# Routing stage of a two-block transformer kernel: whole-u logits, both halves of u turned to tokens, the few experts' columns gathered half by half

## The chip, the cores and the metric

One Trainium2 chip, one core. The time is the device time of one execution in microseconds (us). The core's engines run their own instruction streams and meet at semaphores: TensorE (PE, with its weight loads PEld), VectorE (DVE), ScalarE (ACT), GpSimd (POOL, not used here) and SyncE (SP), which issues the weight transfers.

## The reference, cut to what matters

The model has two blocks of two layers each, on 256 tokens of width 1024, in float32. The last feed-forward of the second block is a mixture of 8 experts with 2 chosen for each token:

```
h = rms_norm_2(x, norm_ffn_g) * (1.0 + sc2) + sh2
logits = h @ router_w                       # 256 x 8
top_v, top_i = lax.top_k(logits, 2)
probs = jax.nn.softmax(top_v, axis=-1)
gates = sum(one_hot(top_i, 8) * probs[..., None], axis=-2)
for e in range(8):
    out = out + gates[..., e:e+1] * ((silu(h @ w1[e]) * (h @ w3[e])) @ w2[e])
x = x + g2 * out
```

Everything before it (three mixing branches, convolutional feed-forwards, linear attention, one dense feed-forward) is not touched.

## The kernel before

Activations lie transposed: `u` is 8 tiles `k` of 128 channels x 256 tokens. A large product is made of three matmuls in the type fp32r: every operand is cut into a high half (rounded to fp32r) and a low half (what is left), and high x high, high x low and low x high are added (`mm3`). For the weights, SP loads units of 128 x 1024 (512 KB) into a ring of 6 buffers, ACT rounds each unit to `w_high` (`high_to`, L1672), DVE subtracts to get `w_low` (`low_to`, L2176), and PE uses the pair. The split units have 6 buffers of their own. A ring buffer is free when the low half is made, a split buffer when PE has multiplied the unit. All orders are written out by hand: every engine's program is a fixed list, and the named steps in `STEPS` are counted by semaphores.

The routing stage stands between the last normalization and the experts:

- The normalization (`rms`, DVE L2217; ACT L1716 and L1719). For each `k` DVE makes `normed`, ACT makes `u_high`, then the whole `u` in float32 (written over `sq`, the first 2048 columns of the arena), and DVE makes `u_low`.
- `route` on PE. The logits are `u_high` and `u_low` times the router in full float32, 32 matmuls of 8 columns (8 tiles `k`, two halves of the tokens, two parts). Then `by_token0` and `by_token1` turn the whole `u` to token rows (8 transposes each, L1502). Between them stand five small matmuls (`counts`), which count how many tokens each expert has.
- DVE meanwhile takes the two best experts of each token (`second`, `chosen`). After `counts` it sorts the experts by their number of tokens (`order`), and makes `pick`, a 0/1 matrix tokens x slots for four groups of 128 slots, and `spread_tok`, its transpose with the gates.
- SP waits for `order` before it loads the first unit of an expert (L3103), since the order says which expert's weights come first.
- `few0` to `few7` gather: `u_tok` (float32) times `pick` (float32) gives 128 x 512 columns in one bank for each `k`. ACT rounds each to `few_high` (L2055), DVE subtracts to get `few_low` (L2208).
- The experts. The three with the most tokens run on all 256 tokens (18 passes of 6 units, `q` = 0 to 17), the other five on gathered slots (30 passes). `up(q)` multiplies 4 units, `turn` transposes the hidden tile, `down` multiplies 2 units.
- After `up(0)` stands `route_back`: 10 transposes of `spread_tok` (L1527), which ACT takes out as `spread_slot` (L2062). They are needed from the first gathered expert on.
- ACT's and DVE's programs for the experts begin with pass 1: first the Silu of pass 0 (L2074) and `hidden`, then the four units of `up(1)`.

Functions are shown below with the line numbers of the profile before.

## Time and profile before

| | us |
|---|---|
| median of 3 timed runs | 2533.5 (2531.13 to 2535.11) |
| the profiled execution's own time | 2517.57 |
| its span | 2516.1 |
| PE busy | 2304.6 (92% of the span) |
| DVE busy | 1596.2 (63%) |
| ACT busy | 1178.8 (47%) |
| DMA, mean | 170 GB/s |
| normalization and routing, from the last squares to the first full-rate pass | 1896 to 1963 |

The page has PE at the head of the chain that ended last (77% of the span), then DVE (14%) and ACT (4%). A float32 matmul (4 passes over the array) is recorded as two instructions, so 64 records are 32 matmuls; fp32r matmuls have one record each. A matmul's duration covers its way through the array and overlaps with the next one's; what one costs in a stream is the distance from start to start. "PEclk" is the granted clock of PE: 0.50 is 1.2 GHz, 1.00 is 2.4 GHz.

### The profile page before, as it was taken

What the parts mean: (1) busy time and instruction counts of PE and PEld (TensorE: products, weight loads), DVE (VectorE), ACT (ScalarE), POOL (GpSimd) and SP (SyncE); (2) the same over time, 40 slices, a digit from 0 to 9 for tenths busy, and PEclk for the clock granted to TensorE, in tenths of its full rate; (3) what the DMA queues carried; (4) which work ended last, traced back from release to release, by engine and by line L of the source; (5) the groups of instructions that cost most, each with busy time, mean ns of one, the idle gap of its engine ahead of it and who ended that gap; (6) DMA issues with size and microseconds to landing.
All of it is one profiled execution on the core that took longest, in us unless ns stands there. A gap on an engine that the chain in (4) does not pass through costs nothing.

```text
span 2516.1 us, 45037 instructions
## 1 busy us (share of the span) xinstructions
PE 2304.6 (92%) x19087; PEld 2076.5 (83%) x19087; DVE 1596.2 (63%) x2425; ACT 1178.8 (47%) x1717; POOL 0.2 (0%) x4
## 2 busy tenths in 40 slices
PE   7889788899988887988998989999989999999998
PEld 7669788899976777888998979998977788887776
DVE  5537776677763687576775656555654444568886
ACT  5234534455552355355554435445333434456665
POOL 0000000000000000000000000000000000000000
PEclk9999898999999999899998989999987999999999
DMA  5674333355446533253553414554312555569895
GB/s 201 224 257 157 113 106 105 130 183 191 139 173 261 197 118 116 86 175 121 193 192 100 134 59 168 185 190 137 118 34 84 184 176 183 190 237 324 321 330 197
DMA packets 118634, 427.06 MB, mean 170 GB/s; under 512 B 13344, under 2 KB 16160, under 8 KB 118304
## 3 DMA queue, kind: packets, MB, share of 16 engines
q1 hardware_dynamic: 116544, 422.34, 48.9%
q8 instruction: 150, 2.46, 0.4%
q10 hardware_dynamic: 1888, 1.84, 0.2%
q14 instruction: 52, 0.43, 0.0%
HBM read 423.08 MB, written 1.05 MB: 169 GB/s over the span
## 4 chain that ended last, share of the span: by engine, by line
PE 77%; DVE 14%; ACT 4%; issue 2%; DMA 2%; ACTq 0%; SPq 0%; DVEq 0%
PE bank L764 76%; DVE w_low L2176 4%; DVE arena L2208 4%; DMA ring<-in_weights 1%; DVE arena L2217 1%; DVE y_mix L2208 1%; ACT w_high L1672 1%; DVE arena L2678 1%; PE bank L1562 1%; ACT arena L1935 1%; DVE small L2676 0%; DVE arena L2214 0%; DVE arena L2212 0%; DVE arena L2227 0%; ACT arena L1880 0%
## 5 line engine op out<-in xcount | busy, mean ns | idle before, releaser
L2176 DVE TENSOR_TENSOR w_low<-ring,w_high 128x1024 fp32r<-128x1024 f32 x700 | 820.1, 1220 | 146.8 <-ACT w_high L1672 146.7
L764 PE MATMUL bank<-u_high,w_high 128*128 128x256 f32 x2576 | 743.0, 288 | 30.0 <-DVE u_low L2208 23.3
L1672 ACT ACTIVATE w_high<-ring 128x1024 fp32r<-128x1024 f32 x700 | 696.0, 1050 | 134.3 <-PE bank L764 128.0
L764 PE MATMUL bank<-u_low,w_high 128*128 128x256 f32 x2576 | 735.1, 285 | 0.0
L764 PE MATMUL bank<-u_high,w_low 128*128 128x256 f32 x2576 | 734.3, 285 | 0.0
L764 PEld LDWEIGHTS bank<-u_high,w_high 128*128 128x128 f32 x2576 | 499.7, 194 | 42.5 <-issue 39.5
L764 PEld LDWEIGHTS bank<-u_low,w_high 128*128 128x128 f32 x2576 | 499.7, 194 | 0.1
L764 PEld LDWEIGHTS bank<-u_high,w_low 128*128 128x128 f32 x2576 | 498.9, 194 | 0.0
L764 PE MATMUL bank<-arena 64*64 64x64 f32 (+8 forms) x4488 | 258.3, 253 | 78.8 <-DVE arena L2217 22.8
L764 PEld LDWEIGHTS bank<-arena 64*64 64x64 f32 (+3 forms) x4488 | 218.9, 154 | 124.7 <-issue 66.5
L764 PE MATMUL bank<-w_high,u_high 128*128 128x256 f32 (+1 forms) x480 | 166.5, 347 | 5.1 <-DVE w_low L2176 5.1
L2208 DVE TENSOR_TENSOR arena<-arena 128x256 f32<-128x256 f32 (+4 forms) x215 | 139.4, 665 | 46.3 <-ACT arena L1981 21.3
L764 PE MATMUL bank<-hid_high,w_high 128*128 128x256 f32 x528 | 150.0, 284 | 15.3 <-DVE hid_low L2208 15.3
L764 PE MATMUL bank<-w_high,u_low 128*128 128x256 f32 (+1 forms) x480 | 163.1, 340 | 0.0
L764 PE MATMUL bank<-w_low,u_high 128*128 128x256 f32 (+1 forms) x480 | 162.8, 339 | 0.0
L764 PE MATMUL bank<-hid_low,w_high 128*128 128x256 f32 x528 | 149.5, 283 | 0.0
L764 PE MATMUL bank<-hid_high,w_low 128*128 128x256 f32 x528 | 149.3, 283 | 0.0
L2208 DVE TENSOR_TENSOR turned_low<-bank,turned_high 128x256 fp32r<-128x256 f32 (+1 forms) x66 | 24.9, 399 | 161.4 <-ACT turned_high L2084 161.4
L2084 ACT ACTIVATE turned_high<-bank 128x256 fp32r<-128x256 f32 (+1 forms) x66 | 22.2, 365 | 223.6 <-PE bank L1562 223.6
L2217 DVE SCALAR_TENSOR_TENSOR arena<-bank,params,arena 128x255 f32<-128x255 f32 (+1 forms) x204 | 85.6, 476 | 50.5 <-ACT arena L1979 32.1
L1678 ACT ACTIVATE arena<-bank 128x512 f32<-128x512 f32 (+1 forms) x72 | 42.1, 584 | 159.8 <-PE bank L764 159.7
L764 PEld LDWEIGHTS bank<-hid_high,w_high 128*128 128x128 f32 x528 | 101.7, 193 | 16.4 <-issue 16.4
(281 smaller groups left out, 3091.1 us busy)
## 6 DMA issues: line engine op xcount, KB each, us to landing
ring<-in_weights SPq DMA_DIRECT2D x534, 512.0 KB, 4.5
ring<-in_moe SPq DMA_DIRECT2D x264, 512.0 KB, 5.3
const<-in_const SPq DMA_DIRECT2D x1, 2619.0 KB, 16.2
x_res<-in_x SPq DMA_DIRECT2D x2, 512.0 KB, 4.8
out<-x_res ACTq DMA_DIRECT2D x2, 512.0 KB, 3.0
const<-in_par ACTq DMA_DIRECT2D x1, 462.0 KB, 3.4
params<-in_par ACTq DMA_DIRECT2D x1, 247.0 KB, 7.9
small<-in_pos SPq DMA_DIRECT2D x1, 128.0 KB, 16.0
```

The lines of the kernel that those rows point to most:

```text
L764: return pe.matmul(out, lhsT, rhs, start=start, stop=stop, skip_group_check=loose)
L1562: ins = pe.transpose(bank(q, tile)[:, f * P:(f + 1) * P], hid_e[q % 2][tile][:, f * P:(f + 1) * P], c_("ident"))
L1672: act.activation(WH[:, ORDER.slot[cut], :], weights("s", cut), Copy).then_inc(s_hi, 1)
L1678: act.activation(job.dst, held(job), Copy).then_inc(s_out["act"], 1)
L1935: act.activation(L_c[a][:, h, :], L_c[a][:, h, :], Exp, bias=neg_max[a][:, h:h + 1], accum_out=exp_sum[a][:, h:h + 1]).then_inc(*c.mark(f" ...
L2084: act.activation(HTH[q % 2][tile][:, 0:n], psum[4 + 2 * (q % 2) + tile][:, 0:n], Copy)\
L2176: dve.tensor_tensor(WL[:, b, :], weights("s", cut), WH[:, b, :].bitcast(f32), SUB).then_inc(s_lo, 1)
L2208: dve.tensor_tensor(out, a, b, op).then_inc(*t.mark(name))
L2217: dve.scalar_tensor_tensor(out, a, s, b, op0, op1).then_inc(*t.mark(name))
L2678: dve.match_replace(work_[:, a, 0:n], top8, work_[:, a, 0:n], -3e30).then_inc(*d.mark())
```

## The change

- The whole `u` is made first for all `k` (`u0` to `u7`), then `u_high` for all `k`; on DVE all eight `normed` come first, then all `u_low`.
- The logits are whole `u` times the router: 16 float32 matmuls.
- `u_high` and `u_low` are both turned to token rows (32 transposes, four groups of 8, in banks 4 to 7) and written as fp32r to `U_TOK` by ACT, 8 copies of 128 x 512. The counts stand between the second group and the third.
- The gather is made of 32 fp32r matmuls: 16 results (`few0` to `few15`), of which 0 to 7 are the high halves and 8 to 15 the low halves. They go through 8 banks, so the last eight wait until an earlier result has been taken out (`X_BANK`).
- The even results are copied by ACT, the odd ones by DVE. The four units of `up(0)` are split between them, and two units of `up(1)` at the end.
- ACT runs a Silu on one column after the Exp, and `spread_slot` is taken out after the Silu of pass 0.
- `silu_e` lies elsewhere in the arena, and `pick` is of type fp32r.

```diff
@@ STEPS @@
-        "logits by_token0 counts by_token1 few0 ... few7 spread0 spread1 spread2",
+        "logits by_token0 by_token1 counts by_token2 by_token3 few0 ... few15 spread0 spread1 spread2",
@@ build @@
+    U_TOK = [pairs2(over_arena(f"by_token_{n}", 8 * T * h, 2048)) for h, n in enumerate(("high", "low"))]
+    X_FEW = [(XH, XL)[n // 8][:, n % 8, :] for n in range(16)]
+    X_BANK = (0, 1, 2, 3, 4, 5, 6, 7, 4, 5, 6, 7, 0, 1, 2, 3)
+    TOK_BANK = ((4, 5), (6, 7), (4, 5), (6, 7))
@@ PE route @@
-                pe.wait_ge(*R.dve(f"low{k}"))
+                pe.wait_ge(*E.act(f"u{k}"))
                 for a in TWO:
-                    for part in (UH, UL):
-                        ins = mm(psum[1][:, a * 8:a * 8 + 8], part[:, k, a * P:(a + 1) * P].bitcast(f32), rw[:, k, :], ...)
+                    ins = mm(psum[1][:, a * 8:a * 8 + 8], sq[:, k, a * P:(a + 1) * P], rw[:, k, :], ...)
...
+            pe.wait_ge(*R.dve(f"low{KT - 1}"))
+            by_token(0, 0)
+            by_token(0, 1)
             pe.wait_ge(*E.dve("chosen"))
...
-            by_token(1)
+            pe.wait_ge(*E.act("tok3"))
+            by_token(1, 0)
+            by_token(1, 1)
             pe.wait_ge(*E.dve("pick"))
-            pe.wait_ge(*E.act("by_token"))
-            for k in range(KT):
+            pe.wait_ge(*E.act("tok7"))
+            for n in range(16):
+                if n > 7:
+                    old = X_BANK.index(X_BANK[n])
+                    pe.wait_ge(*(E.act, E.dve)[old % 2](f"x{old}"))
                 for a in TWO:
-                    ins = mm(psum[k][:, :], u_tok[:, a, k * P:(k + 1) * P], pick[:, a, :], a == 0, a == 1)
+                    ins = mm(psum[X_BANK[n]][:, :], U_TOK[n // 8][:, a, (n % 8) * P:(n % 8 + 1) * P], pick[:, a, :], ...)
@@ PE experts, up @@
-                        pe.wait_ge(*E.dve(f"low{5 + 2 * q}"))
+                        pe.wait_ge(*E.act(f"x{8 + 2 * q}"))
+                        pe.wait_ge(*E.dve(f"x{9 + 2 * q}"))
@@ ACT route @@
+            by_token(0)
+            by_token(1)
             act.wait_ge(*E.dve("second"))
             act.activation(r_p1, r_p1, Exp).then_inc(*E.act.mark("second"))
+            act.activation(unused, eps, Silu).then_inc(*E.act.mark())
+            for n in range(2, 8):
+                by_token(n)
+            for n in range(0, 16, 2):
+                act.wait_ge(*E.pe(f"few{n}"))
+                act.activation(X_FEW[n], psum[X_BANK[n]][:, :], Copy).then_inc(*E.act.mark(f"x{n}"))
+                if n in (2, 6, 10, 12):
+                    high_to(ORDER.up[0][(2, 6, 10, 12).index(n)])
+            high_to(ORDER.up[1][1])
@@ ACT experts @@
                 silu(q - 1)
+                if q == 1:
+                    route_back(of_route)
@@ DVE route @@
-            for k in range(KT):
-                dve.wait_ge(*E.act(f"high{k}"))
-                tt(d, XL[:, k, :], psum[k][:, :], XH[:, k, :].bitcast(f32), SUB, f"low{k}")
-                if k in (3, 5, 7):
-                    low_to(ORDER.up[0][k // 2 - 1])
-            low_to(ORDER.up[0][3])
+            for n in range(1, 16, 2):
+                dve.wait_ge(*E.pe(f"few{n}"))
+                copy(d, X_FEW[n], psum[X_BANK[n]][:, :], f"x{n}")
+                if n in (3, 7, 11, 13):
+                    low_to(ORDER.up[0][(3, 7, 11, 13).index(n)])
+            low_to(ORDER.up[1][1])
```

On PE, from the logits to the first unit of `up(0)`, the kernel before has this (the pair of router rows stands 16 times in all; `arena` is `u_tok`, `const` the identity):

```order
L764 MATMUL bank<-router,u_high 128x8
L764 MATMUL bank<-router,u_low 128x8
L1502 MATMUL bank<-const,arena 128x128 x8
L764 MATMUL bank<-small,steady 128x8 x2
L764 MATMUL bank<-small,const 128x8
L764 MATMUL bank<-small,steady 128x8
L764 MATMUL bank<-small,const 128x8
L1502 MATMUL bank<-const,arena 128x128 x8
L764 MATMUL bank<-arena 128x512 x16
L764 MATMUL bank<-w_high,u_high 128x512
```

The changed kernel has this:

```order
L777 MATMUL bank<-steady,arena 128x1 x10
L777 MATMUL bank<-const,rstd 128x128 x2
L777 MATMUL bank<-router,arena 128x8 x16
L1515 MATMUL bank<-const,u_high 128x128 x16
L777 MATMUL bank<-small,steady 128x8 x2
L777 MATMUL bank<-small,const 128x8
L777 MATMUL bank<-small,steady 128x8
L777 MATMUL bank<-small,const 128x8
L1515 MATMUL bank<-const,u_low 128x128 x16
L777 MATMUL bank<-few_pick,by_token_high 128x512 x16
L777 MATMUL bank<-few_pick,by_token_low 128x512 x16
L777 MATMUL bank<-w_high,u_high 128x512
```

The router rows have become one run of 16. The transposes stand in two groups of 16, the first of `u_high`, the second of `u_low`, and the first 16 gather matmuls read the high halves.

On ACT, from the last `u_high` to the second unit of `up(0)`, the kernel before has this (L2051 takes the token rows out, L2055 the gathered columns):

```order
L1716 ACTIVATE u_high<-arena,mod 128x256
L1719 ACTIVATE arena<-arena,mod 128x256
L2048 ACT_TABLE_LOAD
L2048 ACTIVATE small<-small 128x2
L2051 ACTIVATE arena<-bank 128x512 x4
L2055 ACTIVATE few_high<-bank 128x512 x4
L1672 ACTIVATE w_high<-ring 128x1024
L2055 ACTIVATE few_high<-bank 128x512 x2
L1672 ACTIVATE w_high<-ring 128x1024
L2055 ACTIVATE few_high<-bank 128x512 x2
L1672 ACTIVATE w_high<-ring 128x1024 x2
```

The changed kernel has this, from the whole `u` on (L1734 makes it, L2071 takes out token rows, L2083 gathered columns, L1693 splits units):

```order
L1734 ACTIVATE arena<-arena,mod 128x256 x8
L1740 ACTIVATE u_high<-arena,mod 128x256 x8
L2071 ACTIVATE by_token_high<-bank 128x512 x2
L2077 ACT_TABLE_LOAD
L2077 ACTIVATE small<-small 128x2
L2078 ACT_TABLE_LOAD
L2078 ACTIVATE steady<-steady 128x1
L2071 ACTIVATE by_token_high<-bank 128x512 x2
L2071 ACTIVATE by_token_low<-bank 128x512 x4
L2083 ACTIVATE few_high<-bank 128x512 x2
L1693 ACTIVATE w_high<-ring 128x1024
L2083 ACTIVATE few_high<-bank 128x512 x2
```

Two copies of token rows now stand ahead of the Exp (L2077) and its table load, and a second table load (L2078, for the Silu) stands between them and the other six.

Further down on ACT, around the end of `up(0)`, the kernel before has this (L2062 is `spread_slot`, L2074 the Silu of pass 0, L2084 the turned hidden tile):

```order
L1672 ACTIVATE w_high<-ring 128x1024 x2
L2062 ACTIVATE arena<-bank 128x512 x2
L2062 ACTIVATE arena<-bank 128x256
L2074 ACT_TABLE_LOAD
L2074 ACTIVATE arena<-bank 128x256 x2
L1672 ACTIVATE w_high<-ring 128x1024 x4
L2084 ACTIVATE turned_high_61<-bank 128x256
L2084 ACTIVATE turned_high_62<-bank 128x256
```

The changed kernel has this (L2104 is the Silu, L2092 `spread_slot`, L2114 the turned tile):

```order
L1693 ACTIVATE w_high<-ring 128x1024
L2083 ACTIVATE few_low<-bank 128x512
L1693 ACTIVATE w_high<-ring 128x1024 x2
L2104 ACTIVATE arena<-bank 128x256 x2
L2092 ACTIVATE arena<-bank 128x512 x2
L2092 ACTIVATE arena<-bank 128x256
L1693 ACTIVATE w_high<-ring 128x1024 x2
L2114 ACTIVATE turned_high_64<-bank 128x256
L2114 ACTIVATE turned_high_65<-bank 128x256
```

The first two units of `up(1)` have moved ahead of the Silu and of `spread_slot`, and the table load is gone from here.

## Rows read from the trace of the kernel before

**Rows 1.** Page: PE's busy us, share, instructions; unit splits' busy, mean ns, idle.
```profile
PE 2304.6 (92%) x19087; PEld 2076.5 (83%) x19087; DVE 1596.2 (63%) x2425; ACT 1178.8 (47%) x1717; POOL 0.2 (0%) x4
...
L2176 DVE TENSOR_TENSOR w_low<-ring,w_high 128x1024 fp32r<-128x1024 f32 x700 | 820.1, 1220 | 146.8 <-ACT w_high L1672 146.7
...
L1672 ACT ACTIVATE w_high<-ring 128x1024 fp32r<-128x1024 f32 x700 | 696.0, 1050 | 134.3 <-PE bank L764 128.0
```

**Rows 2.** Busy time of each engine by stretch, then granted clock, DMA share, GB/s.
```profile
1896.00:1950.00 54.00, 47.75 (x183) 36.02 (x183) 27.05 (x84) 19.16 (x36) 0.00 (x0) 0.75 0.28 98
...
1956.00:2260.00 304.00, 303.85 (x1399) 247.33 (x1398) 159.50 (x190) 130.39 (x189) 0.00 (x0) 0.99 0.56 195
```

**Rows 3.** Chain of waits, 1880 to 2000 us: start, duration, work.
```profile
1899.08 13.82 PE bank L764 x64
...
1955.49 7.76 PE bank L764 x24
...
1963.69 16.80 PE bank L764 x72
```

**Rows 4.** Timeline of PE, 1896 to 1960 us: start, duration, work, [idle before].
```profile
1912.76 1.95 PE L1502 MATMUL bank<-const,arena 128*128 128x128 f32 x8
1914.62 1.02 PE L764 MATMUL bank<-small,steady 128*128 128x8 f32 x4
...
1922.69 15.43 PE L764 MATMUL bank<-arena 128*128 128x512 f32 x32 [3.96 <-DVE arena L2217]
...
1949.18 1.25 PE L1527 MATMUL bank<-const,arena 128*128 128x128 f32 x10
1955.49 0.77 PE L764 MATMUL bank<-w_high,u_high 128*128 128x512 f32 x1 [5.06 <-DVE w_low L2176]
1956.06 0.63 PE L764 MATMUL bank<-w_low,u_high 128*128 128x512 f32 x1
...
1959.04 0.63 PE L764 MATMUL bank<-w_high,u_low 128*128 128x512 f32 x1
```

**Rows 5.** Timeline of ACT, 1896 to 1960 us.
```profile
1898.00 0.51 ACT L1716 ACTIVATE u_high<-arena,mod 128x256 fp32r<-128x256 f32 x1 [1.61 <-DVE arena L2217]
...
1904.51 1.28 ACT L2048 ACT_TABLE_LOAD   x1
...
1914.74 1.08 ACT L2051 ACTIVATE arena<-bank 128x512 f32<-128x512 f32 x2 [0.65 <-PE bank L1502]
...
1926.14 0.60 ACT L2055 ACTIVATE few_high<-bank 128x512 fp32r<-128x512 f32 x1 [6.29 <-PE bank L764]
...
1949.81 1.36 ACT L2062 ACTIVATE arena<-bank 128x512 f32<-128x512 f32 x3 [9.16 <-PE bank L1527]
1951.19 1.28 ACT L2074 ACT_TABLE_LOAD   x1
1952.49 0.66 ACT L2074 ACTIVATE arena<-bank 128x256 f32<-128x256 f32 x2
```

**Rows 6.** Timeline of DVE, 1896 to 1960 us.
```profile
1916.96 0.17 DVE L2217 SCALAR_TENSOR_TENSOR small<-bank,const 128x8 f32<-128x8 f32 x1 [1.41 <-PE bank L764]
...
1922.55 2.65 DVE L2214 TENSOR_SCALAR arena<-const,small 128x128 f32<-128x128 f32 x10
1926.77 0.69 DVE L2208 TENSOR_TENSOR few_low<-bank,few_high 128x512 fp32r<-128x512 f32 x1 [1.56 <-ACT few_high L2055]
```

**Rows 7.** Timeline of SP's DMA queue, 1917 to 1926 us.
```profile
1918.65 3.00 SPq L3109 DMA_DIRECT2D ring<-in_moe  x6
```

**Rows 8.** Busy time by stretch, around the steps of PE's granted clock.
```profile
1898.00:1899.00 1.00, 0.00 (x0) 0.00 (x0) 0.82 (x3) 1.00 (x3) 0.00 (x0) 0.65 0.00 0
...
1925.00:1926.00 1.00, 1.00 (x3) 0.35 (x2) 0.20 (x1) 0.00 (x0) 0.00 (x0) 0.70 0.94 356
1928.00:1930.00 2.00, 2.00 (x6) 0.95 (x5) 0.69 (x1) 0.88 (x2) 0.00 (x0) 1.00 0.22 88
1959.00:1960.00 1.00, 1.00 (x4) 0.82 (x3) 0.00 (x0) 0.00 (x0) 0.00 (x0) 0.63 0.72 270
```

More of the change, by code:

```diff
@@ L368 @@
         "normed7 low6 low7",
+    "ffn3_pe":
+        "sum spread",
+    "ffn3_act":
+        "-1 sq0 sq1 sq2 sq3 sq4 sq5 sq6 sq7 root high0 high1 high2 high3 high4 high5 high6 high7",
+    "ffn3_dve":
+        "inverse normed0 normed1 normed2 normed3 normed4 normed5 normed6 normed7 low0 low1 low2 low3 low4 "
+        "low5 low6 low7",
     "add2_pe":
@@ L411 @@
     "route_pe":
-        "logits by_token0 counts by_token1 few0 few1 few2 few3 few4 few5 few6 few7 spread0 spread1 spread2",
+        "logits by_token0 by_token1 counts by_token2 by_token3 few0 few1 few2 few3 few4 few5 few6 few7 few8 "
+        "few9 few10 few11 few12 few13 few14 few15 spread0 spread1 spread2",
     "route_act":
-        "-7 u second -3 by_token high0 high1 high2 high3 high4 high5 high6 high7 spread0 spread1 spread2",
+        "u0 u1 u2 u3 u4 u5 u6 u7 tok0 tok1 second -1 tok2 tok3 tok4 tok5 tok6 tok7 x0 x2 x4 x6 x8 x10 x12 x14 "
+        "spread0 spread1 spread2",
     "route_dve":
-        "-5 second -3 chosen -8 order -22 pick -9 spread low0 low1 low2 low3 low4 low5 low6 low7",
+        "-5 second -3 chosen -8 order -22 pick -9 spread x1 x3 x5 x7 x9 x11 x13 x15",
     "tables_act":
@@ L688, in build @@
     space(8 * T)
-    u_tok = pairs2(new(2048))
-    back = u_tok
+    back = pairs2(new(2048))
     XH, XL = (over_arena(n, 16 * T + 4096 * h, 4096).rearrange("p (k s) -> p k s", k=KT)
@@ L709, in build @@
     of_conv = [[stage("conv", layer * FF_GROUPS + j) for j in range(FF_GROUPS)] for layer in range(LAYERS)]
-    of_mix2, of_lin, of_ffn2 = (
-        [stage(name, layer) for layer in range(LAYERS)] for name in ("mix2", "lin", "ffn2"))
+    of_mix2, of_lin = (
+        [stage(name, layer) for layer in range(LAYERS)] for name in ("mix2", "lin"))
+    of_ffn2 = [stage("ffn2", 0), stage("ffn3", 0)]
     of_add2 = stage("add2", 0)
@@ L1574, in down @@
                     pe.wait_ge(*E.act("spread2"))
-                    pe.wait_ge(*E.dve("low3"))
                 for tile in tiles(q):
@@ L1710, in rms @@
         def rms(R, add_of=None, whole=None):
+            for k in range(KT) if whole is not None else ():
+                act.wait_ge(*R.dve(f"normed{k}"))
+                act.activation(sq[:, k, :], un[:, k, :], Ident, bias=add_of(k)).then_inc(*whole.act.mark(f"u{k}"))
             for k in range(KT):
@@ L2265, in rms @@
                 stt(d, out[:, k, :], X[:, k, :], g_of(k), mean_of(R), MUL, MUL, f"normed{k}")
-                if k and out is un:
+                if k and out is un and R is not of_ffn2[-1]:
                     low(R, k - 1, un, add_of)
-            if out is un:
-                low(R, KT - 1, un, add_of)
+            for k in range(KT) if R is of_ffn2[-1] else (KT - 1,) if out is un else ():
+                low(R, k, un, add_of)
         def branch_a(A, M, side, layer):
```

51 lines of the change are left out of this document (23 added, 28 removed).

## Prediction, made before the changed kernel was run

> **What bounds the kernel now.** I read the page first, then busy time by stretch. PE is busy for 92% of the span, so it bounds the kernel as a whole [rows 1]. Around the change this is different: from 1896 to 1950 us PE is "busy" for 47.75 of 54 us, but at a mean granted clock of 0.75, with DMA at a share of 0.28, while the expert passes behind it keep PE busy for 303.85 of 304 us at 0.99 [rows 2]. So the routing stage is a serial piece in which PE either waits or runs slowly. What it saves passes to the end: the passes that follow hang on PE alone, and each is 16.80 us for 72 matmuls, 0.233 us each [rows 3].
>
> The chain of waits and the timelines then give the stage's order: `u` ready, logits 1899.08 to 1912.76, transposes and counts, DVE's sorting until `pick`, gather from 1922.69, `up(0)`, `route_back` at 1949.18, and 5.06 us of waiting for `w_low` before `up(1)` starts at 1955.49 [rows 3, 4, 6]. `up(0)` is 48 matmuls, so it began 48 x 0.233 = 11.2 us before 1949.18, at 1938.0.
>
> **Logits.** 32 matmuls took 1912.76 - 1899.08 = 13.7 us, 0.427 each, at 1.2 GHz: the clock fell during 1898 to 1899, when PE had nothing to do [rows 4, 8]. Sixteen are left, 6.8 us. They start when the first whole `u` is there. Before, the first logits waited for `normed`, high (0.51) and low on DVE; now for one ACTIVATE after `normed`, which ends at 1898.5 [rows 5]. ACT makes 16 of these in 6.5 us, 0.40 each [rows 5]; two matmuls for each `k` take 0.85, so PE sets the pace. Logits end at 1898.55 + 6.83 = 1905.4, 7.4 us earlier. The reordered halves don't hold them: high0 comes after u7, at 1901.2, and low7 ends at 1905.0, just ahead of the wait in front of the first transposes. If that wait came out 0.5 us late, this would cost 0.5.
>
> **Transposes and counts.** Eight transposes take 1.86 us (1912.76 to 1914.62) [rows 4]. Sixteen now stand ahead of the counts: 1905.4 + 3.72 = 1909.1. From the first count to DVE's next step were 2.34 us (1914.62 to 1916.96) [rows 4, 6], so DVE goes on at 1911.45, 5.5 us earlier than before. Is it free by then? ACT takes out two token copies first (they began 1.98 us after the first transpose and took 1.08 [rows 4, 5]: until 1908.5), then the Exp's table load, 1.28 [rows 5], which earlier lay in idle time at 1904.51; the Exp ends at 1910.0. DVE's six small steps for the gates come behind it; all 18 small steps between logits and counts took 2.8 us before (1912.76 until 1.41 before 1916.96 [rows 4, 6]), so 1.1 us is my estimate for the six: 1911.1. The margin is 0.35 us. From there to `pick` are 5.7 us as before (1916.96 to the gather's release at 1922.69) [rows 4, 6]: ready at 1917.15. SP's first six expert loads move with it, from 1918.65 to 1913.1 [rows 7].
>
> **The second half of the tokens.** After the Exp comes the Silu's table load with its one-column Silu (0.2, an estimate below the 0.33 of a 256-column one in row 1952.49), 1.5 us: until 1911.5. The next two copies end at 1912.6. PE waits for them (`tok3`), turns `u_low` from 1912.6 to 1916.3, and ACT's last copy (`tok7`) ends at 1917.5. That is 0.4 us after `pick`, so the token copies now release the gather, at 1917.5 instead of 1922.69: 5.2 us gained here. The chain from the logits to this point goes through ACT, and what ACT takes longer than I say comes on top one for one.
>
> The table loads are where a page speaks against this change. The trace has a load at 1951.19 directly behind an ACTIVATE row that ends at 1951.17, and the Silu behind the load at 1952.49: 1.28 in all with no gap on either side [rows 5]. The Trainium skill ("ScalarE: Activation LUTs", section "What ACT_TABLE_LOAD costs") puts a switch of sets at 1283 ns for the load and about 1380 ns for a drain. By that rule the loads' duration agrees and the drain doesn't show. With the drain twice on the new path the gather would start 2.8 us later. I go by the row.
>
> **The gather.** In float32, 16 matmuls took from 1922.69 to 1938.0, 15.3 us; the first result went to ACT at 1926.14, after two matmuls of 1.7 us [rows 4, 5]. Now there are 32 fp32r matmuls of 512 columns, a form that `up` shows at both clocks: 0.426 from start to start between 1956.06 and 1959.04 (seven of them), 0.233 at full clock [rows 3, 4]. Bounds for this term are 32 x 0.233 = 7.5 us (full clock from the start) and 32 x 0.427 = 13.7 us (low throughout). In between: after PE took up dense work at 1922.69, the clock rose at about 1925.6 (0.70 in that microsecond), and after 1955.49 at about 1959.7 (0.63 in that one) [rows 8], so 2.9 and 4.3 us. The gather's first matmuls have the form of the second case, so I take 4.3 us: 10 matmuls at 0.427 and 22 at 0.233, 9.4 us, until 1926.9.
>
> Can ACT and DVE follow? A copy on ACT is 0.60 and on DVE about 0.69 (that of `few_low` from a bank; the copy has the same 128 x 512) [rows 5, 6]. DVE has the ten `spread_tok` steps first, 2.65 [rows 6], until 1919.7; few1 is then just done. Walking both programs with units of 1.05 (ACT) and 1.22 (DVE) [rows 1]: x5 is out at 1923.7, when `few9` wants its bank after `few8` at 1923.7; x7 at 1924.3 before `few11`; x9, for which `up(0)` waits, at 1925.9. So `few15` ends at 1927.0 with next to nothing lost. Low halves of `up(0)`'s units come at 1923.1, 1925.4, 1927.6 and 1929.3, and PE wants them at 1927.0, 1929.8, 1932.6 and 1935.4. The loads: before, DMA fell to a share of 0.22 in 1928 to 1930, so six units had landed some 10 us after 1918.65 [rows 7, 8]; now that is by 1923.5, and the fourth unit is first touched at 1926.7. `up(0)` starts at 1927.0 instead of 1938.0: 11.0 us gained so far.
>
> **`route_back` and `up(1)`.** Before, ACT took `spread_slot` out, loaded the Silu's table, ran the Silu, and only then split the first unit of `up(1)`; PE waited 5.06 us [rows 4, 5]. Now both first units are split by 1932, ahead of the end of `up(0)` at 1938.2. That wait goes. What is late next? PE goes from `route_back` (10 transposes, 1.25) at 1939.4 straight into 24 matmuls; the second two units need their high halves, which ACT makes after the Silu (0.66) and `spread_slot` (1.36, from 1939.6): they are split by 1944.6 on DVE, and PE wants them at 1945.5. So nothing. The wait also let the clock fall: the 24 matmuls took 7.76 us [rows 3] against 24 x 0.233 = 5.6. Those 2.2 us go too, if the clock stays up.
>
> **Sum.** End of the first half of `up(1)`: 1963.25 before, 1927.0 + 11.2 + 1.25 + 5.6 = 1945.05 now. By terms: 5.2 (gather starts) + 5.8 (gather shorter) + 5.06 (wait) + 2.2 (clock) = 18.2 us. Against the profiled execution, 2517.57, this gives 2499.4. The median of the timed runs lies 15.9 us above the profiled time; I carry the difference over: 2533.5 - 18.2 = 2515.3.
>
> **Rivals.**
>
> A, a table switch costs more than its load, as in the page above, or ACT is late otherwise: the gather starts at 1920.3, saving 15.4, 2518.1. The row speaks against it. 8%.
>
> B, the clock stays at 1.2 GHz for the whole gather. For it: the last eight results wait for banks, and transposes and copies ahead leave PE gaps. Price 13.7 - 9.4 = 4.3, and half of `up(0)` at the low clock another 24 x 0.193 = 4.6. Saving 9.3 to 13.9: 2519.6 to 2524.2. Against: the float32 gather and `up(1)` both brought the clock back within 4.3 us [rows 8], and the walk above finds no bank wait over 0.1 us. The Trainium skill ("TensorE: Matmul & The Clock Gate", section "A second HAM failure mode: psum-queue depth-cycling") tells of a kernel whose cycling through PSUM banks left short idle times and a clock that went up and down; the gather now cycles through banks in this way, and no row of before has such cycling with fp32r matmuls. 13%.
>
> C, slower: the clock stays low through the gather, `up(0)`, `route_back` and `up(1)`. Gather 13.7, `up(0)` 20.5, ten transposes 2.3, 24 matmuls 10.2: from 1917.5 to 1964.2, 1 us behind the 1963.25 of before, and each further pass of 72 adds 13.9. It decides if the clock is not up by about 1964; with one more pass 2533.5 + 1.0 + 13.9 = 2548.4. `up(0)` has no bank to wait for, and dense passes always raised the clock [rows 2, 8]. 2%.
>
> D, more is saved: the clock rises right at the gather's start, or doesn't fall for the logits. Then the gather's end is held by x9 at 1925.9 and the transposes lose up to 3.5 us, of which ACT's copies leave about 1. Saving 19 to 20.5: 2513 to 2514.5. 7%.
>
> E, the stage is shorter but the saving is given back behind it: the gathered experts load more than the dense ones, and a memory bound there would not move. But loads are tied to the ring's buffers, so they move with PE, and nothing has a fixed time. A saving under 5 us: 2528.5 to 2533.5. 4%.
>
> The forecast, a saving of 16.5 to 19, has 66%.
>
> **How the numbers follow.** Likeliest 2515. The range holds A, D, most of B, and some 2 us in which a median may differ: 2510 to 2523. About 0.2% (5 us) is what a measurement of this kernel can tell from no change: faster takes the forecast, A, B and D, 94%, less 1 for what I haven't seen, 93%; same is E, 4%; slower is C and the unseen, 3%.
>
> **What would show it.** In the changed profile: 32 router records (16 matmuls) over 6.8 us; gather starting 17 to 20 us after the logits' start (19.0 by my sum); few results from start to end in 9 to 10 us; no wait above 1 us between `up(0)` and `up(1)`; first half of `up(1)` in 5.6 us. It would be wrong if the gather's matmuls stood 0.427 apart to the end, if a gap stood around the table loads, or if `up(0)` waited for a copy on DVE.

## The result and the profile after

| | before | after |
|---|---|---|
| median with the prediction's comparison | 2534.06 us (4 runs) | 2509.28 us (2508.04 to 2515.12, 4 runs) |
| ratio, 95% interval | | 0.9905 [0.9888, 0.9923] |
| repeated | | 0.9914 [0.9892, 0.9936] and 0.9931 [0.9910, 0.9952] |
| all executions in this study, mean and standard error | 2531.6, 0.5 (75 executions, 2522.6 to 2543.9) | 2510.3, 1.1 (16, 2504.2 to 2519.0) |
| profiled execution's span | 2516.1 | 2506.6 |
| the routing stage in it | 66.51 | 48.54 |

The change makes the kernel faster, as forecast, but the median fell just below the range (2510 to 2523). "Stage" is here the time from the start of the spread of the last normalization's roots to the end of the first half of `up(1)` in the chain of waits: 1896.74 to 1963.25 us before [rows 3] and 1904.09 to 1952.63 after. The "spread" is the step in which PE copies each token's root to all rows, just ahead of the whole `u`. It is this row of the chain before:

```profile
1896.74 0.72 PE bank L764 x4
```

PE's timeline of the changed kernel (start, duration, work, idle before), with the rows that answer to [rows 4]:

```profile
1904.09 0.71 PE L777 MATMUL bank<-const,rstd 128*128 128x128 f32 x4 [0.65 <-DVE rstd L2255]
1905.92 7.00 PE L777 MATMUL bank<-router,arena 128*128 128x8 f32 x32 [1.11 <-ACT arena L1734]
1912.76 3.36 PE L1515 MATMUL bank<-const,u_high 128*128 128x128 f32 x16
...
1919.89 3.67 PE L1515 MATMUL bank<-const,u_low 128*128 128x128 f32 x16 [2.75 <-ACT by_token_high L2071]
1924.83 6.00 PE L777 MATMUL bank<-few_pick,by_token_high 128*128 128x512 f32 x16 [1.27 <-DVE arena L2246]
1930.67 4.07 PE L777 MATMUL bank<-few_pick,by_token_low 128*128 128x512 f32 x16
...
1945.78 1.25 PE L1548 MATMUL bank<-const,arena 128*128 128x128 f32 x10
...
1952.47 0.60 PE L1584 MATMUL bank<-const,arena 128*128 128x128 f32 x4
```

The 16 logits matmuls (32 records) take 1912.76 - 1905.92 = 6.84 us against 13.7. From the logits' start to the gather's are 18.91 us against 23.61. The gather runs from 1924.83 to 1934.58 (48 x 0.233 ahead of 1945.78), 9.75 us against 15.3. `route_back` goes into `up(1)` with no wait.

The chain of waits (start, duration, work) shows the end of it, with 24 matmuls in 5.60 us where [rows 3] had 7.76:

```profile
1924.83 21.11 PE bank L777 x80
...
1947.03 5.60 PE bank L777 x24
```

ACT's timeline, for [rows 5], and DVE's, for [rows 6]:

```profile
1914.75 1.09 ACT L2071 ACTIVATE by_token_high<-bank 128x512 fp32r<-128x512 f32 x2 [2.90 <-PE bank L1515]
1915.85 1.28 ACT L2077 ACT_TABLE_LOAD   x1
1917.15 0.20 ACT L2077 ACTIVATE small<-small 128x2 f32<-128x2 f32 x1
1917.37 1.28 ACT L2078 ACT_TABLE_LOAD   x1
1918.66 0.20 ACT L2078 ACTIVATE steady<-steady 128x1 f32<-128x1 f32 x1
1918.77 1.07 ACT L2071 ACTIVATE by_token_high<-bank 128x512 fp32r<-128x512 f32 x2
...
1923.60 1.09 ACT L2071 ACTIVATE by_token_low<-bank 128x512 fp32r<-128x512 f32 x2 [0.62 <-PE bank L1515]
```

```profile
1909.09 3.27 DVE L2249 SCALAR_TENSOR_TENSOR u_low<-arena,mod,u_high 128x256 fp32r<-128x256 f32 x8 [1.02 <-ACT u_high L1740]
...
1917.38 0.17 DVE L2244 TENSOR_SCALAR small<-small 128x2 f32<-128x2 f32 x1 [2.80 <-ACT small L2077]
...
1918.37 0.16 DVE L2249 SCALAR_TENSOR_TENSOR small<-bank,const 128x8 f32<-128x8 f32 x1
...
1923.42 0.61 DVE L2249 SCALAR_TENSOR_TENSOR few_pick<-const,small,few_pick 128x128 fp32r<-128x128 f32 x2
1923.96 2.65 DVE L2246 TENSOR_SCALAR arena<-const,small 128x128 f32<-128x128 f32 x10
```

Two table loads of 1.28 us stand on ACT with nothing on either side of them but the ACTIVATEs. DVE waited 2.80 us for the Exp and used the counts, which were there, as soon as the gates were done. The last token copies ended at 1924.69, after `pick` at 1924.03, and the gather began at 1924.83. (Its row names DVE's L2246 as the releaser, which makes `spread_tok` and which the gather doesn't wait for; the same row of after_again, below, names the token copies.)

Busy time by stretch, with the granted clock in the third place from the end, around the clock's steps, for [rows 8]:

```profile
1905.00:1906.00 1.00, 0.08 (x1) 0.09 (x1) 1.00 (x3) 0.65 (x2) 0.00 (x0) 0.72 0.00 0
1915.00:1916.00 1.00, 1.00 (x9) 1.00 (x7) 0.00 (x0) 0.98 (x3) 0.00 (x0) 0.66 0.00 0
1919.00:1920.00 1.00, 0.11 (x1) 0.11 (x2) 0.86 (x7) 0.84 (x2) 0.00 (x0) 0.55 0.00 0
1929.00:1930.00 1.00, 1.00 (x6) 0.77 (x5) 0.97 (x2) 0.84 (x2) 0.00 (x0) 0.83 0.60 242
```

The clock falls at about 1905.4, in the idle time between the spread and the logits, rises in the first group of transposes at about 1915.7, falls again at about 1919.1, 2.0 us into the 2.75 us in which PE stood idle, and rises at about 1929.3, 4.5 us into the gather. Before, it stayed low from 1898.3, ahead of the logits, until 1925.6.

### The profile page after: what moved, and what is told of

The parts are those of the page before. It is cut to its first block, busy times and chain, and to the rows that moved or that the text cites. A ratio compares the mean times of both kernels' runs of the same rounds, so it can differ in the third digit from the quotient of the medians.

```text
span 2506.6 us, 45010 instructions
## 1 busy us (share of the span) xinstructions
PE 2296.7 (92%) x19071; PEld 2075.5 (83%) x19071; DVE 1595.7 (64%) x2425; ACT 1181.1 (47%) x1722; POOL 0.2 (0%) x4
## 4 chain that ended last, share of the span: by engine, by line
PE 78%; DVE 14%; ACT 4%; issue 3%; DMA 2%; ACTq 0%; SPq 0%; DVEq 0%
PE bank L777 76%; DVE w_low L2208 4%; DVE arena L2240 4%; DMA ring<-in_weights 1%; DVE arena L2249 1%; DVE y_mix L2240 1%; ACT w_high L1693 1%; DVE arena L2710 1%; PE bank L1584 1%; ACT arena L1956 1%; DVE arena L2246 0%; DVE small L2708 0%; DVE arena L2259 0%; DVE arena L2244 0%; ACT arena L1901 0%
## 5 line engine op out<-in xcount | busy, mean ns | idle before, releaser
L1693 ACT ACTIVATE w_high<-ring 128x1024 fp32r<-128x1024 f32 x700 | 696.5, 1050 | 132.0 <-PE bank L777 125.3
L777 PE MATMUL bank<-arena 64*64 64x64 f32 (+5 forms) x4456 | 245.1, 251 | 79.9 <-issue 23.1
L777 PEld LDWEIGHTS bank<-arena 64*64 64x64 f32 (+2 forms) x4456 | 214.5, 155 | 117.4 <-issue 63.3
L2240 DVE TENSOR_TENSOR arena<-arena 128x256 f32<-128x256 f32 (+4 forms) x215 | 139.4, 665 | 46.3 <-ACT arena L2002 21.3
L777 PE MATMUL bank<-hid_high,w_high 128*128 128x256 f32 x528 | 150.1, 284 | 15.3 <-DVE hid_low L2240 15.3
L2114 ACT ACTIVATE turned_high<-bank 128x256 fp32r<-128x256 f32 (+1 forms) x66 | 22.2, 365 | 218.9 <-PE bank L1584 218.9
## 6 DMA issues: line engine op xcount, KB each, us to landing
small<-in_pos SPq DMA_DIRECT2D x1, 128.0 KB, 15.9
```

The lines of the kernel that those rows point to most:

```text
L777: return pe.matmul(out, lhsT, rhs, start=start, stop=stop, skip_group_check=loose)
L1693: act.activation(WH[:, ORDER.slot[cut], :], weights("s", cut), Copy).then_inc(s_hi, 1)
L2114: act.activation(HTH[q % 2][tile][:, 0:n], psum[4 + 2 * (q % 2) + tile][:, 0:n], Copy)\
L2240: dve.tensor_tensor(out, a, b, op).then_inc(*t.mark(name))
```

## Experiments

Stages are measured as above, times of runs are means with standard errors. The one comparison of all is with before: stage 66.5, mean 2531.6.

**The two kernels again.** No edit.

> The kernel before, unchanged, run as if it were a new one. The profile of before was 2517.57 us, its timed runs 2531 to 2535, and I carried that difference over to the changed kernel. Theory 1: the profiled execution was one draw from a spread that comes from the PE clock in the first 1900 us (each low stretch costs about half its length); the routing stage itself is the same in every execution. Then the profile here shows the stage (from the spread of the last normalization's roots to the end of the first half of up(1)) at 66.5 us, plus or minus 2, and a whole time of 2520 to 2535, with the missing part before the stage. Theory 2: the stage itself is longer in typical runs of before (72 to 75 us, the clock rising later), so that the change is worth 24 us there. Rival: before has no spread, and an execution of it is at 2517 whenever it is profiled and at 2531 when it is not; then all profiles are some 15 us under the timed runs.

> The kernel before again, for one more profile. Two profiles of it have the stage at 66.5 us and the unchanged work ahead of it at 1896.7 and 1912.6 us. If the part ahead is what varies: stage 66.5 again, start of the stage anywhere from 1895 to 1917. If before's own stage is longer in typical executions (that would explain why timed means of changed kernels lie some 4 us further below before than their stages do): 68 us or more, by a longer low stretch in the gather, as in tail_alone's profile (30.7 us low, gather 16.9).

> As before_p3: one more profile of the kernel before. Stage 66.5 by the one view, 68 us or more by the other.

> The changed kernel again, beside before. Theory 1: the stage is 48.5 us (measured in the first profile), plus or minus 2, and what differs between executions lies ahead of it; timed ratio 0.990 to 0.993. Theory 2: ratio 0.990 with a stage of 48.5 and one of before of over 70.

> The changed kernel once more, for its stage and its mean. If what the timed runs show beyond the stage (21.9 against 18.0 to 19.6 us so far) is the scatter of the unchanged part: stage 46.9 to 48.6 us, mean of the runs 2510 to 2514, so that the difference to before comes down towards 18 to 20. If it is a lasting gain outside the stage: mean 2509 to 2510 again and a difference of 21 to 23.

| profile of | stage starts at | stage | rest behind it | span | mean clock of the execution |
|---|---|---|---|---|---|
| before, first | 1896.74 | 66.51 | 552.9 | 2516.1 | 0.951 |
| before_again | 1912.55 | 66.48 | 552.9 | 2531.9 | 0.944 |
| before_p3 | 1905.85 | 66.55 | 553.5 | 2525.9 | 0.946 |
| before_p4 | 1909.78 | 66.69 | 552.5 | 2529.0 | 0.945 |
| after, first | 1904.09 | 48.54 | 554.0 | 2506.6 | 0.951 |
| after_again | 1908.79 | 46.95 | 552.8 | 2508.5 | 0.947 |
| after_p3 | 1904.63 | 46.93 | 552.7 | 2504.3 | 0.951 |

The chain of waits in before_again, at its start and end of the stage:

```profile
1912.55 0.72 PE bank L764 x4
...
1971.27 7.76 PE bank L764 x24
```

The stage of before is the same within 0.2 us in four profiles, so theory 2 of the first expectation fell, and so did the rival: before_again's own profiled execution took 2533.39. What varies is the unchanged work ahead of the stage, by 16 us, and the mean clock of PE varies with it: 0.951 over 2516 us is 2 x 0.049 x 2516 = 247 us at the low clock, 0.944 over 2532 is 284. Half of the 37 us between them is 18, against 15.8 measured. The profile on which I built the forecast was faster than all 75 executions of before in this study.

The changed kernel's stage comes in two lengths, 48.5 and 46.9 us, and the gather makes 1.3 of the 1.6 between them: it takes 9.75 us in the first profile, 8.44 in the other two. PE's timeline in after_again:

```profile
1929.23 3.91 PE L777 MATMUL bank<-few_pick,by_token_high 128*128 128x512 f32 x16 [1.26 <-ACT by_token_low L2071]
1932.98 0.73 PE L777 MATMUL bank<-few_pick,by_token_low 128*128 128x512 f32 x2
1934.36 3.48 PE L777 MATMUL bank<-few_pick,by_token_low 128*128 128x512 f32 x14 [0.64 <-DVE few_high L2252]
```

There the clock fell at about 1924.1 and was up again at about 1927.5, before the gather began (a mean of 0.74 from 1927 to 1928, 1.00 from 1928 on), so the second low stretch took 3.4 us and not 10.2. At the full clock the gather still took 8.44 us and not 7.5, since PE waited 0.64 us for a bank that DVE was late to empty: DVE's ten `spread_tok` steps lasted until 1931.3. after_p3 has the same rows, with the same 0.64.

**One part alone, on the kernel before.** In logits_alone only the logits come from the whole `u`:

```diff
-                pe.wait_ge(*R.dve(f"low{k}"))
-                    for part in (UH, UL): (two matmuls)
+                pe.wait_ge(*E.act("u" if k == KT - 1 else f"u{k}"))
+                    (one matmul on sq[:, k, ...])
```

> The kernel before with one part of the change alone: the logits from whole u (16 matmuls that wait for u of their k), all else as before. If the term is 16 matmuls of 0.427 us and nothing else: logits 6.8 us instead of 13.7, stage 66.5 - 6.8 = 59.6 us (less 0.1 or so for the earlier start), all later pieces unchanged, time 7 us less than before. Rival: the low clock stretch, 27.3 us long in both profiles of before, ends or moves with the shorter piece, so that the transposes and the gather come out at the full clock and the part is worth 10 us or more.

Its PE timeline:

```profile
1908.62 6.99 PE L764 MATMUL bank<-router,arena 128*128 128x8 f32 x32 [1.51 <-ACT arena L1718]
...
1925.40 15.50 PE L764 MATMUL bank<-arena 128*128 128x512 f32 x32 [3.96 <-DVE arena L2216]
```

Stage 59.67, 6.8 us less, as the sum said; the gather still takes its 15.3 us, with the low clock at its start. Mean 2521.1 (1.2), 10.5 below before, 3.7 (1.3) more than the stage gives.

In tail_alone only the tail is changed (early Silu, `spread_slot` behind the first Silu, two units of `up(1)` ahead, and `silu_e` elsewhere in the arena):

```diff
+            act.activation(unused, eps, Silu)          # behind the Exp
-            high_to(ORDER.up[0][3])
+            high_to(ORDER.up[1][1])                    # DVE: low_to, the same
+                if q == 1: route_back(of_route)        # behind silu(0)
```

> The kernel before with only the tail changed: early Silu on one column, spread_slot behind the Silu of pass 0, two units of up(1) split ahead. By the forecast 5.06 us of waiting and 2.2 us of low clock go: stage 59.2 us, time 7.3 less than before. undo_tail gave 7.4 to 9.0 us of stage in the changed kernel. Rival: the Silu's load, 1.28 us, now stands between the Exp and the token copies and delays the gather, 6.0 us net.

```profile
1937.46 17.07 PE L764 MATMUL bank<-arena 128*128 128x512 f32 x32 [3.96 <-DVE arena L2222]
```

The gather still starts 23.60 us after the logits, so the Silu's load costs nothing there. But its 32 records take 17.07 us against 15.43 [rows 4]: the clock rose 6.2 us into it in this execution, against 2.9 before. Stage 60.94; without that 1.65 us it would be 59.3 by this reckoning, the 7.2 us of the sum; this is worked out, not measured. Mean 2521.7 (1.2).

**One part undone, on the changed kernel.** undo_tail takes the same lines back:

> Changed kernel with the tail as before: no early Silu, spread_slot taken out ahead of the Silu, the units of up(1) split only behind it. By my sum 5.1 us of waiting and 2.2 us of low clock come back: stage 55.7 us, time 7.2 us more than the changed kernel. Rival: with the gather shorter, ACT has idle time and the wait is covered: under 2 us.

```profile
1948.63 1.25 PE L1548 MATMUL bank<-const,arena 128*128 128x128 f32 x10
...
1954.94 0.77 PE L777 MATMUL bank<-w_high,u_high 128*128 128x512 f32 x1 [5.06 <-DVE w_low L2203]
...
1963.04 0.60 PE L1584 MATMUL bank<-const,arena 128*128 128x128 f32 x4
```

Stage 55.75 against the 55.7 expected: the wait of 5.06 us for `w_low` is back to the hundredth, and the 24 matmuls behind it take 8.1 us. The clock was low for the first 5.5 us of its gather, so the profile of the changed kernel to set beside it is the first, and the part is worth 7.2. Mean 2518.5 (1.0), 8.2 above the changed kernel.

undo_logits computes the logits from the halves again, in the changed order:

```diff
-                pe.wait_ge(*E.act(f"u{k}"))
+                pe.wait_ge(*R.dve(f"low{k}"))
+                    for part in (UH, UL): (two matmuls)
```

> The changed kernel with the logits from the two halves (32 matmuls, waiting for each low half). By the sum: logits 13.7 us instead of 6.8, and they start at the first low half, 2.8 us later than at the first whole u, since the changed order has all highs behind all u: stage 9 to 10 us longer (56 to 58), time 9 to 10 us more. Rival: only 6.8 us, as in logits_alone the other way round.

```profile
1912.92 0.71 PE L777 MATMUL bank<-const,rstd 128*128 128x128 f32 x4 [0.65 <-DVE rstd L2256]
1918.46 0.59 PE L777 MATMUL bank<-router,u_high 128*128 128x8 f32 x2 [4.82 <-DVE u_low L2250]
...
1932.13 3.32 PE L1516 MATMUL bank<-const,u_high 128*128 128x128 f32 x16
```

Stage 59.05, 10.5 to 12.1 more than the changed kernel's (10.5 against the first profile, whose gather had the clock low as long as here), a little over the 9 to 10: the logits take 13.67 and start 5.54 us after the spread instead of 1.83, 3.7 later where I had 2.8. Mean 2521.3 (1.6), 11.0 more. With logits that need the halves, the new order (all highs behind all `u`) costs 3.2 us against before, where they started 2.34 us after the spread.

**The gather.** gather_f32 keeps everything but the type:

```diff
-    pick = pairs2(over_arena("few_pick", pick_at, 2 * 4 * P))
+    pick = pairs2(at(pick_at, 2 * 4 * P))
-    U_TOK = [pairs2(over_arena(f"by_token_{n}", 8 * T * h, 2048)) ...]
+    U_TOK = [pairs2(at(8 * T * h, 2048)) for h in TWO]
```

> The changed kernel with the turned halves and pick in float32, so that the 32 gather matmuls run in float32 (0.86 us each at the full clock, by before's gather) instead of fp32r. By the sum the type is what pays for gathering twice: gather 28 to 31 us instead of 8.4 to 9.8, stage 67 to 70, time about 2529 to 2532, no better than before. Rival: copies and banks set the gather's pace, and it grows by less than 15 us.

```profile
1924.68 27.71 PE L777 MATMUL bank<-arena 128*128 128x512 f32 x64 [1.26 <-ACT arena L2071]
```

The row has the 64 records of the 32 matmuls. From 1924.68 to `up(0)` are 27.5 us, 0.86 a matmul, and the stage is 65.99. Mean 2529.7 (1.1): nearly all that the change brings is gone. In fp32r a gather matmul of 512 columns takes 0.233 us where one in float32 takes 0.86, so twice the matmuls still take 8.4 to 9.75 us against 15.3.

No run gathers the old way with the rest of the change in place, so what doubling the gather is worth with all that comes with it (16 more transposes, four more token copies, the new order) is shown by no run. An estimate from the stages, if the parts add: before less logits_alone's 6.8 and the tail's 7.2 is 52.4, and the changed kernel has 46.9 to 48.5, so 4 to 5.5 us. From the other side it is nothing: 48.5 plus 10.5 (undo_logits) plus 7.2 (undo_tail) is 66.3, against 66.5 of before. The gather in halves seems to pay only together with the logits from the whole `u`.

one_engine has ACT copy all 16 results:

```diff
-            for n in range(0, 16, 2):
+            for n in range(16):        # ACT; DVE's copies go
```

> The changed kernel with all 16 gathered results copied by ACT; DVE only splits. ACT then has 16 x 0.50 + 4 x 1.05 = 12.2 us from the first result on, before the last result; x8 and x9 come out about 8 us after the first result. By my walk banks for few8 to few15 come later and up(0) waits for x9: gather to up(0) 11 to 12 us instead of 8.4 to 9.8, and the units of up(0), split in between, come just in time; stage 1.5 to 3 us longer. Rival (the clock sets the gather's length): the same stage within 0.5 us.

```profile
1928.21 3.88 PE L777 MATMUL bank<-few_pick,by_token_high 128*128 128x512 f32 x16 [1.27 <-DVE arena L2246]
1932.49 1.72 PE L777 MATMUL bank<-few_pick,by_token_low 128*128 128x512 f32 x6 [0.40 <-ACT few_high L2083]
1934.89 2.60 PE L777 MATMUL bank<-few_pick,by_token_low 128*128 128x512 f32 x10 [0.69 <-ACT few_high L2083]
```

PE waited 0.40 and 0.69 us for banks; gather 9.12 us, stage 47.69, mean 2509.5 (0.9, 4 runs). The clock was up before this gather began, as in after_again and after_p3, so those are the ones to compare with: 0.7 us more than their 8.44, where I had expected 1.5 to 3. The second engine matters little: with it PE still waits 0.64 us for a bank, without it 1.09.

**What holds the changed stage.** exp_first moves the Exp:

```diff
-            by_token(0)
-            by_token(1)
             act.wait_ge(*E.dve("second"))
             act.activation(r_p1, r_p1, Exp)
+            for n in range(4):
+                by_token(n)
             act.activation(unused, eps, Silu)
-            for n in range(2, 8):
+            for n in range(4, 8):
```

> Changed kernel with ACT's Exp ahead of the token copies (its table load in the idle time ahead of the logits' end) and the Silu's load behind the fourth copy. In the changed kernel's profile DVE waited 2.80 us for the Exp, and PE 2.75 us for the fourth copy. If these waits are the path: pick 1.3 us earlier, u_low's transposes 2.6 earlier, gather starts 2.0 us earlier, stage 46.5 us, time 2 us less. Rival (the counts on PE would hold DVE anyway, since they come behind 16 transposes): under 0.5 us.

```profile
1916.57 1.97 PE L1515 MATMUL bank<-const,u_low 128*128 128x128 f32 x16 [0.16 <-ACT by_token_high L2071]
1922.17 5.42 PE L777 MATMUL bank<-few_pick,by_token_high 128*128 128x512 f32 x16 [3.64 <-DVE few_pick L2249]
...
1928.60 3.48 PE L777 MATMUL bank<-few_pick,by_token_low 128*128 128x512 f32 x14 [0.54 <-DVE few_high L2252]
```

The waits went (2.75 us for the copy became 0.16) and the gather began 17.21 us after the logits instead of 18.91 or 18.6, 1.4 to 1.7 of the 2.0 expected. PE now waited 3.64 us for `pick`. The clock fell at about 1922.0, at the end of that idle time, and rose at about 1925.4:

```profile
1919.00:1921.00 2.00, 0.00 (x0) 0.00 (x0) 1.86 (x12) 0.97 (x2) 0.00 (x0) 1.00 0.92 307
1921.00:1923.00 2.00, 0.83 (x2) 0.73 (x3) 1.97 (x9) 0.00 (x0) 0.00 (x0) 0.75 0.97 324
...
1925.00:1927.00 2.00, 2.00 (x10) 1.61 (x9) 1.26 (x3) 1.86 (x3) 0.00 (x0) 0.89 0.99 391
```

The gather took 9.75 us, with the clock low for its first 3.3 and the wait of 0.54 for a bank, so the stage, 46.86, is no better than the better profiles of the changed kernel; mean 2510.7 (1.7).

evict_first is exp_first with two changes more: it also puts `spread_tok` behind DVE's copies, and each unit of `up(0)` one pair of results later.

> exp_first with DVE's ten spread_tok steps (2.65 us) behind the copies of gathered columns, and each unit of up(0) split one pair of results later, since few9 waited 0.54 us for x5 in exp_first. If banks hold the gather: gather 9.2 us instead of 9.75 at the same clock, stage 46.2. If the clock alone sets the gather's length: 9.7 to 9.8, or 8.4 to 8.5 when the low stretch is 3.4 us; no change in the stage.

Gather 8.81 us, below the 9.2 of the first view and between the two cases of the second; stage 45.70. No wait for a bank is left in it, and the clock was low for its first 3.0 us, nearly as long as in exp_first, so most of the 0.9 us between the two is what waiting for banks cost there. Mean 2511.1 (1.1).

evict_first_warm is evict_first with one more change: it fills the idle time in front of the gather (evict_warm_2 is the same kernel again):

```diff
+        def busy(n):
+            for _ in range(n):
+                mm(psum[3][:, 0:256], UH[:, 0, 0:P], UH[:, 0, :], True, True)
             by_token(1, 1)
+            busy(24)
             pe.wait_ge(*E.dve("pick"))
```

> evict_first with 24 fp32r matmuls of 256 columns, whose result nobody reads, on PE between the last transposes and the gather, where PE was idle for 3.6 us in exp_first (24 x 0.117 = 2.8 us at the full clock, 5.1 at the low one). If the idle time is what lets the clock fall in front of the gather: no low stretch behind the first one, gather 7.6 to 8.6 us, stage 44.5 to 45.5, time 1 to 2 us less than evict_first. Rival: the clock is low there already, the fill runs 5.1 us and pushes the gather back: stage 1 to 2 us longer.

> evict_first_warm again beside the changed kernel on one chip. Its stage was 44.3 us against 48.5 and 46.9 of the changed kernel; the timed runs of the first call did not show it (2509.2). If the stage's gain passes to the end: stage 44.0 to 44.6, and 2.5 to 4 us less than the changed kernel here. If it is given back in the unchanged part: no difference in the means.

PE's timeline and the clock of evict_warm_2:

```profile
1920.27 1.97 PE L1519 MATMUL bank<-const,u_low 128*128 128x128 f32 x16 [0.16 <-ACT by_token_high L2077]
1922.00 3.11 PE L777 MATMUL bank<-u_high 128*128 128x256 f32 x24
1925.87 3.93 PE L777 MATMUL bank<-few_pick,by_token_high 128*128 128x512 f32 x16 [0.77 <-DVE few_pick L2255]
1929.64 3.80 PE L777 MATMUL bank<-few_pick,by_token_low 128*128 128x512 f32 x16
```

```profile
1919.00:1923.00 4.00, 3.84 (x35) 3.75 (x35) 2.54 (x15) 3.84 (x7) 0.00 (x0) 1.00 0.07 10
1923.00:1927.00 4.00, 3.23 (x23) 2.85 (x22) 2.67 (x13) 1.05 (x3) 0.00 (x0) 1.00 0.87 298
```

The clock stays at 1.00 and the gather takes 7.40 us, the 32 x 0.233 that was the lower bound; stage 44.27 and 44.49. In the two profiles with this order and no fill (exp_first and evict_first) the clock fell ahead of the gather; in the three with it (these two and warm_all) it did not. That the idle time lets it fall is shown for this order, on these five profiles. The changed kernel's own gather was held by the clock in one profile of three and by a bank in the other two, so the 7.40 needed both changes. Their worth in the whole time is not shown: mean 2509.4 (0.9) over 12 executions against 2510.3 (1.1) for the changed kernel; the stages differ by 3.1. Against before it is 0.9917 [0.9898, 0.9935] and 0.9924 [0.9910, 0.9937]. It has, with warm_all, the shortest stage of all that I ran, and I can't say that it beats the changed kernel.

warm_all is evict_first_warm and fills the idle times around the spread too (with 3 and 5 float32 matmuls of 128 columns), and puts one 128-column float32 matmul that nobody reads behind each pair of logits matmuls but the last.

> evict_first_warm with more matmuls that nobody reads: 3 and 5 float32 ones of 128 columns in the two idle times around the spread of the roots, and one behind the two logits matmuls of each k. In all profiles the clock fell 1.1 to 1.9 us after the spread and stayed low for 10.2 us, through the logits. If wide matmuls between the narrow ones keep it up: no low stretch, logits with their fill 5.1 us, then DVE's low7 (8.3 us after the spread) holds the copy of the logits, so only the transposes and counts gain: stage 42.5 to 43.5. Rival: the fill does not keep the clock up, and the logits with their fill take 16 x 0.427 + 7 x 0.43 = 9.8 us: stage 47.

```profile
1915.00:1920.00 5.00, 5.00 (x43) 4.75 (x43) 3.39 (x9) 3.39 (x9) 0.00 (x0) 1.00 0.01 3
1920.00:1925.00 5.00, 5.00 (x28) 5.00 (x29) 3.83 (x13) 4.58 (x10) 0.00 (x0) 0.57 0.01 2
```

The clock fell all the same, only later: at about 1920.7, 3.3 us into the logits, while PE was busy without a gap. The logits with their fill took 6.8 us, so nothing was gained before the transposes; stage 44.49, mean 2512.0 (1.2). Neither view held.

## Why the prediction missed

**The stage was right**, in its length and in most of its terms. Forecast 66.5 - 18.2 = 48.3, measured 48.54 in the first profile and 46.9 in two more. Term by term:

| term | forecast | measured (first profile) |
|---|---|---|
| logits' start after the spread | 1.8 | 1.83 |
| logits | 6.83 | 6.84 |
| logits' start to the gather | 19.0 | 18.91 |
| gather to `up(0)` | 9.4 to 9.5 | 9.75 |
| wait ahead of `up(1)` | 0 | 0 |
| first half of `up(1)` | 5.6 | 5.6 |

Shown singly are the logits (logits_alone, 6.8), the tail (undo_tail, 7.2) and the type of the gather (gather_f32, 17.5 to 19). The gather's doubling isn't; it is the estimate above.

**Two steps in it were wrong inside.** I let the counts on PE hold DVE, with a margin of 0.35 us for the Exp. The clock rose in the first group of transposes, which I had priced at the low clock (3.7 us; they took 3.2), so the counts were early and the Exp, behind two copies and a table load, became what DVE waited for. The token copies still released the gather when I said, 18.9 us after the logits; exp_first showed that both waits hung on the same ACT order.

The second is "the walk above finds no bank wait over 0.1 us". I had walked the copies beside a gather whose first 4.3 us are slow. With the clock up from the start, in after_again and after_p3, PE waited 0.64 us for a bank.

**The table switch.** The Trainium skill ("ScalarE: Activation LUTs", "What ACT_TABLE_LOAD costs") adds some 1.38 us of drain to the load's 1.28. On this path it would have shown twice: the Exp started at 1917.15, 1.30 after its load began, the next load 0.02 after the Exp's end, and the copy at 1918.77. The load alone is the price here. Rival A fell.

**The clock.** Rival B, low through the whole gather, fell: the clock rose 4.5 us into it in the first profile (I had taken 4.3), and in after_again and after_p3 it was up 1.7 us before the gather began. Rival C fell with it. Those two profiles are rival D, to which I gave 7%: they save 19.6 us of stage, above my 16.5 to 19. That the first profile agreed with my 4.3 us so closely was luck. Rival E, a saving given back behind the stage, fell too: what follows it takes 552.5 to 554.0 us in all seven profiles. What I had not asked is what fills the gap ahead of the gather: 24 matmuls nobody reads, with the copies in a better order, brought it to its bound.

**The step that failed is the last of the sum:** "The median of the timed runs lies 15.9 us above the profiled time; I carry the difference over: 2533.5 - 18.2 = 2515.3", with "some 2 us in which a median may differ" for the lower end, 2510. The first half treats one fast draw as an offset of the kernel; in fact executions of before scatter over 21 us around 2531.6, in the part ahead of the stage. That alone moves the forecast only to 2531.6 - 18.2 = 2513.4. The 6.0 us between 2515.3 and the measured 2509.28 divide into 1.9 for this offset, 0.8 for a stage that saves 19.0 on average and not 18.2, 2.3 (1.2) that the means save beyond the stage, and 1.0 by which this median of four lies below the mean of all 16, 2510.3. The second half was too small: means of 4 to 6 executions here have standard errors of 1 to 2.6 us on either side, so the lower end belonged at 2507 or so. The mean of all 16 executions lies just inside the range, and the standard error of a mean of four is 1.6, so that this median came out 0.7 us below the range and not above its edge is within the scatter.

**What stays open.** The medians of the first comparison differ by 24.8 us, the means of all executions by 21.3 (1.2), the stages by 18.0 to 19.6. The changed kernel's mean less its stage (47.5 on average) is 2462.8; for before it is 2465.1; for the other kernels, which share the same unchanged work, it runs from 2460.7 (tail_alone) to 2467.5 (warm_all). So 2.3 us (1.2) beyond the stage are of the size by which the unchanged part differs between kernels anyway. The profiles don't settle it: the stage starts at 1906.2 on average in the four of before and at 1905.8 in the three of after, but single ones lie up to 16 us apart. after_p3 settled neither way: stage 46.93, mean 2510.9 (2.6). A lasting gain outside the stage is neither shown nor excluded, and why the unchanged part differs by some us between kernels isn't known.

## What to carry to other kernels

In a serial piece between dense ones, walk the chain with durations at the clock that the rows show; that gave 18.2 us here against 18.0 to 19.6. Walk the copies at the full clock too, since that is where a bank comes late. The gather of the two fp32r halves took 8.4 to 9.75 us against 15.3 for the one in float32, though it has twice the columns; its transposes, copies and order take part of this back (4 to 5.5 us are left, by an estimate). And before a profile's offset to the timed runs is carried over, profile the unchanged kernel again: where the clock decides, one profile is one draw.

## What the runs showed of the hardware

- Logits matmuls of 8 columns in float32 kept PE busy without a gap for 6.84 us (13.7 before), 0.427 us each. The clock had fallen in the idle time ahead of them (at 1905.4, 0.5 us ahead, in the changed kernel; at 1898.3, 0.8 us ahead, before) and stayed at 1.2 GHz through them. In warm_all, with that idle time filled and one 128-column matmul behind every two narrow ones, it fell 3.3 us into them, with PE busy.
- In the 16 transposes of 128 columns behind the logits the clock rose before the last of them ended, in all three profiles of the changed kernel (0.66 in the microsecond from 1915 in the first). In before, with two groups of 8, the counts between them and 4 us of idle time, it stayed low and rose 2.9 us into the gather.
- The clock fell again 2.0 us into an idle time of PE of 2.75 us (after) and 3.5 us into one of 3.64 (exp_first); with that place filled by 24 fp32r matmuls it did not (evict_first_warm, twice). Whether it is back before the gather differs between executions of one kernel: 4.5 us into it in the first profile of after, 1.7 us ahead of it in the other two.
- A gather matmul of 128 x 512 took 0.233 us in fp32r (evict_warm_2) and 0.86 in float32 (gather_f32), both at the full clock.
- An ACT_TABLE_LOAD took 1.28 us, with 0.01 to 0.02 us between it and the ACTIVATEs on either side.
- One program's executions scattered by 21 us (0.8%, 2522.74 to 2543.91 on one chip), and much of it goes with the clock: 0.941 for the slowest execution of before_again (2543.91 us) and 0.945 for its fastest (2524.93), which is 300 against 278 us at the low clock, so some 11 of the 19 us between them; the rounding of the clock leaves 2 or 3 us of doubt in that.
